# The convolution's taps transformed in three 32-row groups of TensorE's array, with a PSUM bank each

## What is computed

```python
def causal_depthwise_conv(x, w):
    """x: (B,T,C), w: (K,C). y[t] = sum_k w[k] * x[t-(K-1)+k] (left zero pad)."""
    k_width, ch = w.shape
    return lax.conv_general_dilated(
        x, w[:, None, :].astype(x.dtype), window_strides=(1,),
        padding=[(k_width - 1, 0)], dimension_numbers=("NWC", "WIO", "NWC"),
        feature_group_count=ch)

def conformer_conv_module(h, w_pw1, b_pw1, w_dw, b_dw, ln_g, ln_b, w_pw2, b_pw2):
    a, g = jnp.split(h @ w_pw1 + b_pw1, 2, axis=-1)
    u = a * jax.nn.sigmoid(g)
    u = causal_depthwise_conv(u, w_dw) + b_dw
    u = jax.nn.silu(layer_norm(u, ln_g, ln_b))
    return u @ w_pw2 + b_pw2
```

## Time and profile before

| | |
|---|---|
| median of three runs | 1133.9 us |
| the profiled execution: its own time | 1135.11 us |
| its span, first to last instruction | 1133.8 us |
| PE busy | 1108.0 us, 98% of the span |
| DVE busy | 758.7 us, 67% |
| ACT busy | 591.3 us, 52% |
| mean granted TensorE clock | 0.991 |
| DMA | 207.74 MB, mean 183 GB/s |

### The profile page before, as it was taken

The page is one execution under the profiler, slowest core; times in us unless marked ns, Lnnn a source line. Parts: engine busy times, 40 slices in busy tenths (PEclk is TensorE's granted clock), DMA queues, the critical chain, the costliest instruction groups (busy, mean ns, idle before and its releaser), DMA issues.

```text
span 1133.8 us, 19190 instructions
## 1 busy us (share of the span) xinstructions
PE 1108.0 (98%) x7742; PEld 1008.6 (89%) x7742; DVE 758.7 (67%) x1414; ACT 591.3 (52%) x1047; POOL 47.3 (4%) x48
## 2 busy tenths in 40 slices
PE   8999999999899999999999999999999999999998
PEld 7998888889699999789987999997889889999986
DVE  2579686997778887776577666664555566666644
ACT  4375474555576666335346754454473267444542
POOL 0160000010000000110000000000000000000000
PEclk9999999999999999999999999999999989999999
DMA  8955952553345554755432655545534234545441
GB/s 327 381 220 207 374 203 86 203 204 149 112 173 183 184 187 168 278 224 186 158 122 75 245 205 178 181 161 202 189 139 139 75 130 166 191 177 181 160 169 38
DMA packets 30796, 207.74 MB, mean 183 GB/s; under 512 B 3539, under 2 KB 4051, under 8 KB 7156
## 3 DMA queue, kind: packets, MB, share of 16 engines
q1 hardware_dynamic: 30708, 206.51, 49.8%
HBM read 205.45 MB, written 1.05 MB: 182 GB/s over the span
## 4 chain that ended last, share of the span: by engine, by line
PE 83%; DVE 10%; ACT 3%; issue 2%; DMA 1%; SPq 0%; ACTq 0%; DVEq 0%
PE ps L401 45%; PE ps L1715 19%; PE ps L635 3%; PE ps L1493 3%; DVE wlo L360 2%; PE ps L419 2%; DVE tm L574 1%; DMA raw<-wa 1%; PE ps L2363 1%; PE ps L2395 1%; ACT whi L352 1%; PE ps L821 1%; PE ps L1842 1%; PE ps L1347 1%; PE ps L432 1%
## 5 line engine op out<-in xcount | busy, mean ns | idle before, releaser
L360 DVE TENSOR_TENSOR wlo<-raw,whi 128x1024 fp32r<-128x1024 f32 (+2 forms) x328 | 372.4, 1177 | 220.4 <-ACT whi L352 219.9
L352 ACT ACTIVATE whi<-raw 128x1024 fp32r<-128x1024 f32 (+2 forms) x328 | 315.5, 1011 | 167.2 <-PE ps L1715 101.4
L401 PE MATMUL ps<-H_h,whi 128*128 128x256 f32 x1376 | 394.3, 287 | 0.0
L401 PE MATMUL ps<-H_h,wlo 128*128 128x256 f32 x1376 | 389.9, 283 | 0.0
L401 PE MATMUL ps<-H_l,whi 128*128 128x256 f32 x1376 | 389.9, 283 | 0.0
L401 PEld LDWEIGHTS ps<-H_h,whi 128*128 128x128 f32 x1376 | 264.8, 192 | 3.3 <-issue 3.0
L401 PEld LDWEIGHTS ps<-H_l,whi 128*128 128x128 f32 x1376 | 264.7, 192 | 0.6 <-issue 0.5
L401 PEld LDWEIGHTS ps<-H_h,wlo 128*128 128x128 f32 x1376 | 264.6, 192 | 0.0
L1715 PE MATMUL ps<-whi,gl_h 128*128 128x512 f32 x264 | 105.6, 400 | 0.5 <-DVE wlo L360 0.5
L1715 PE MATMUL ps<-whi,gl_l 128*128 128x512 f32 x264 | 104.6, 396 | 0.0
L1715 PE MATMUL ps<-wlo,gl_h 128*128 128x512 f32 x264 | 104.6, 396 | 0.0
(11 more groups left out here) (462 smaller groups left out, 1692.1 us busy)
## 6 DMA issues: line engine op xcount, KB each, us to landing
raw<-f SPq DMA_DIRECT2D x44, 1024.0 KB, 4.9
raw<-win SPq DMA_DIRECT2D x27, 1024.0 KB, 6.7
raw<-ada SPq DMA_DIRECT2D x24, 1024.0 KB, 4.9
raw<-up SPq DMA_DIRECT2D x22, 1024.0 KB, 4.8
raw<-g SPq DMA_DIRECT2D x20, 1024.0 KB, 4.9
raw<-pw SPq DMA_DIRECT2D x12, 1024.0 KB, 4.8
raw<-down SPq DMA_DIRECT2D x10, 1024.0 KB, 4.9
raw<-wa SPq DMA_DIRECT2D x4, 1024.0 KB, 10.3
```

The lines of the kernel that those rows point to most:

```text
L352: act.activation(whi[j % NS][:, a:b], raw_of(key)[:, a:b], ACT.Copy).then_inc(w_hi.hit(key, half), 1)
L360: dve.tensor_tensor(wlo[j % NS][:, a:b], raw_of(key)[:, a:b], whi[j % NS][:, a:b].bitcast(F32), ALU.subtract).then_inc(w_lo.hit(key, half), 1)
L401: ins_ = pe.matmul(bank[:, m * 256:(m + 1) * 256], wt[a][:, kt * w + col + m * 128:kt * w + col + m * 128 + 128], act[b][:, k0 + kt, :], s ...
```

## The change

The taps lie three times in `wdw`, from partitions 0, 32 and 64 on, by three loads; the matrix `FW` stands on the same partitions of `dft` (which is loaded whole, as before). The three parts m of one half of the channels are now multiplied one behind the other, part m with the rows from partition 32 m on, so in a 32-row group of the array of its own, and into a bank of its own. PE does half 0 after the gemm of c = 0 and half 1 after that of c = 2, nothing after that of c = 1. ScalarE copies half 0 (four instructions) in its step 1, half 1 (four) in its step 3, nothing in step 2. PE's wait at the mixer's start is for the last of the four loads. The number of matmuls, of copies and their shapes are the same.

```diff
@@ build
-    wdw = sb("wdw", [31, 1024])
+    wdw = sb("wdw", [95, 1024])
@@
-    FW = dft[0:31, 768:1152]
+
+    TAPS = [slice(32 * m, 32 * m + 31) for m in range(3)]
+    FW = [dft[rw, 768 + 128 * m:896 + 128 * m] for m, rw in enumerate(TAPS)]
@@
-    def taps_pe(pe, m, half):
-
-        b, old = M.take(dft_ws(m, half))
-        if old:
-            pe.wait_ge(*old)
-        where["taps", m, half] = b
-        pe.matmul(b[:], FW[:, m * 128:(m + 1) * 128], wdw[:, half * 512:(half + 1) * 512], start=True, stop=True).then_inc(
-            dft_w.hit(m, half), 1)
+    def taps_pe(pe, half):
+
+        for m in range(3):
+            b, old = M.take(dft_ws(m, half))
+            if old:
+                pe.wait_ge(*old)
+            where["taps", m, half] = b
+        for m, rw in enumerate(TAPS):
+            pe.matmul(where["taps", m, half][:], FW[m], wdw[rw, half * 512:(half + 1) * 512], start=True, stop=True).then_inc(
+                dft_w.hit(m, half), 1)
@@ mix1_pe
-        pe.wait_ge(*dft_in(1))
+        pe.wait_ge(*dft_in(3))
@@
-            if c < 3:
-                taps_pe(pe, c, 0)
-                taps_pe(pe, c, 1)
+            if c in (0, 2):
+                taps_pe(pe, c // 2)
@@ mix1_act
-            if 0 < c < 4:
-                taps_act(act, c - 1, 0)
-                taps_act(act, c - 1, 1)
+            if c in (1, 3):
+                for m in range(3):
+                    taps_act(act, m, c // 2)
@@ sp_program
-                sp.dma_start(wdw[:], ins["wdw"]).then_inc(dft_in.hit(1), 16)
+                for m, rw in enumerate(TAPS):
+                    sp.dma_start(wdw[rw, :], ins["wdw"]).then_inc(dft_in.hit(1 + m), 16)
@@ _transforms
-    out[0:31, 768:1152] = np.concatenate([re(f, lag), im(f, lag), last(lag, (re, im, im, re))], 1)
+    for m in range(3):
+        out[32 * m:32 * m + 31, 768:1152] = np.concatenate([re(f, lag), im(f, lag), last(lag, (re, im, im, re))], 1)
```

## The result

The changed kernel takes **1140.45 us** in the median (1139.55 to 1143.13, four runs) against 1134.27 us of the kernel before (1133.64 to 1135.82, four runs): a ratio of 1.0052, with a 95% interval of 1.0041 to 1.0064. It is slower by about 6 us. The forecast was 1130.2, with a range to 1132.6.

The account below looks back on a forecast made before the run. PE was taken to bound the kernel, busy 98% of the span. Its gain of 3.75 us, with copies and loads costing nothing, made 1133.9 us into 1130.2; range 1129.0 to 1132.6.

Parts of the forecast that it names:

- The array: PE's tap matmuls in the mixer: row groups save 3.36 us, one visit fewer 0.39, together 3.75 us.
- The lower end: Tap passes on PE: a group of six costs only its longest part, two passes, 0.86 us, against 2.56 in a row.
- the columns' row: Profile row near the kernel's start: float32 product in four 32-column groups, 32 matmuls in 1.93 us, almost fully at once.
- The rivals on the array: Three alternatives for the tap passes on PE: program order 0.10, row groups not overlapping 0.09, switches draining the array 0.04.
- Strict order: Tap passes on PE start in program order; gain only 2.1 us, 1131.8 us; chance 0.10.
- no overlap: Row groups on PE don't run at once; only the visit's 0.39 us is saved, 1133.5 us; chance 0.09.
- the drain: Each switch between row groups drains PE's array, at 0.39 us a switch; 3.5 us slower, 1137.4 us; chance 0.04.
- the four slots: Time a group of six tap passes needs on PE if started in program order: 1.71 us a group.
- the same share of the ideal: Tap passes on PE: three groups at the skill's four-group share, 2.3 times; passes 2.2 us, gain 3.3 us.
- ScalarE in step 3: Two more copies ahead of `ut`: priced at nothing with 0.8 us slack; as rival, 2 us later gives 1131.4, chance 0.07.
- The loads: Two more tap loads of 124 KB in SP's queue ahead of f0,3: 1.4 us of transfer, covered, costing nothing.
- a wait for a DMA near 650 us: Sign in the changed profile, ahead of the mixer, that the two added loads were not free.

Follow-up runs that it names:

- rows32_serial: rows32 with all three parts reading the first 31 rows, so all six matmuls of a visit share one row group; 1134.36 us.
- rows32_pairs: rows32 with the first two parts in the first row group and the third in the second; 1131.76 us (one run).
- rows32: The changed kernel with the taps padded by a row of zeros, so each of the three loads has 32 rows; 1130.53 us.
- loads_late: The changed kernel with its three loads of 31 rows issued together ahead of f0,11 instead of f0,3; 1130.95 us.
- before_rows32: The kernel before with its one load of the taps padded from 31 to 32 rows; 1134.61 us, ratio 0.9997.
- before_3loads: The kernel before with the changed kernel's three loads of 31 rows, only the first read, array and copies as before; 1143.5 us, ratio 1.0075.

## Why the prediction was wrong

**The array, right.** Two visits with six passes, 1.06 us each in the chain ("some 1.1" in the prediction), 3.79 us gained for 3.75, and in its parts 3.41 for 3.36 and 0.38 for 0.39 (rows32_serial). The lower end was the right choice, and the columns' row was a good guide for rows. What the profile had shown of column groups held: three row groups at once, float32, two passes each.

**The rivals on the array, wrong.** Strict order would have made entries of 1.9 us, no overlap 2.8, the drain more. The rule of strict order of the Trainium skill (TensorE: Matmul & The Clock Gate, Part 3) does not hold for such passes: the entry of 1.06 us has no room for the four slots that the prediction worked out by it, and in rows32_pairs the third part's passes start ahead of the second part's. The 3.07 times that the Trainium skill gives there for four row groups was no bound for the share either: three groups are 2.6 times as fast here (2.77 against 1.06, edges included), where the same share of the ideal would be 2.3.

**ScalarE in step 3, right.** In rows32, where nothing else disturbs, the copy `ut` runs from 852.07 to 852.68 (forecast to 852.55) and the first `forward_pe` begins at 853.63 without waiting for it; 0.95 us of slack, 0.8 were forecast. ScalarE, then PE, in rows32:

```profile
852.07 0.61 ACT L2352 ACTIVATE ut<-ps 128x512 f32<-128x512 f32 x1
```

```profile
853.41 0.38 PE L2345 MATMUL ps<-con_sb,tm 128*128 128x128 f32 x2
853.63 2.76 PE L2367 MATMUL ps<-ut,dft 128*128 128x256 f32 x12
```

**The loads, the step that failed.** The prediction had "two more of 124 KB ... the transfer by 0.25 MB, 1.4 us at the mean 183 GB/s of the run", and f0,3 "landing 4.9 us later in the median, it has 12 us"; "both cost nothing". Three things in it were wrong. *The size:* two loads put the landing off by 12.4 us, not 1.4, because each went through one DMA engine of 16, as loads_late shows. A mean rate over a run says nothing of a transfer of another shape. *The slack:* the median of 44 loads was taken for the one load that mattered, and this one took 13.4 us in the very trace that was read. It had 4.4 us left, not 12. Thirteen microseconds where the load before it, issued at 611.2, took 4.8, directly behind a load of 31 rows, was the sign that could be seen before anything was changed (dft lay in front too; before_rows32 shows that some 6 us were of the 31 rows). *The price of a wait:* 7.5 us of PE standing still cost some 10 in the profile, because the clock was at the lower level for several microseconds after it.

**The side, and the rival that was missing.** The prediction had its rivals on the array and on the copies, where the change is seen, and gave the slower side to a drain of the array. The loads got one paragraph and no rival, although what would show them wrong, "a wait for a DMA near 650 us", was named, and came at 645.6 to 654.2.

**The sum as it was.** Forecast: -3.75. Measured by parts: array -3.8 (rows32 against rows32_serial: 1130.53 against 1134.36), loads +8.6 (before_3loads; 7.0 to 10.0) or 10.2 (the one profile). That makes +4.8 or +6.4, and the kernel is 6.2 slower (4.7 to 7.3).

## What to carry to other kernels

Of a load that is added, ask three things: how many DMA engines its row count can use, what is queued directly behind it, and how long after its own landing that transfer is needed, read from its own row and never from a median. A short, odd-shaped transfer (31 rows) can hold up megabytes behind it; one row of padding removed that here at no cost. And products of 31 rows of contraction, each into its own bank, ran in three row groups at once, so such products should stand next to each other. When two of them share a row group, a third can finish before the second, so a count of finished products doesn't tell which they are.

## What the runs showed of the hardware

A load of 31 rows of 4 KB occupies one DMA engine (6.3% of the 16 engines' time in loads_late) and delays a 1 MB load behind it by 6 us; of 32 rows, by next to nothing (7.2 us to landing behind one load, 7.4 behind three); 95 rows in one load, by 2.7 to 3.7 us more than 96 in three.

PE runs passes of different row groups at once although they end in the same partitions (in different banks), and goes past a pass whose row group is busy to one behind it: six passes in 1.06 us with three groups, in 1.91 with four of them in one group, in 2.77 with all in one.
